# A transformer block pair on one core: the high weights meet high and low activations in one 512-column matmul, and experts are chosen in seven pieces

## The chip, the cores and the metric

The kernel runs on one core of one Trainium2 chip. A core has TensorE (PE, matrix products into PSUM), VectorE (DVE), ScalarE (ACT), GpSimd (POOL), SyncE (SP, which here only starts DMAs) and 16 DMA engines. The metric is the device time of the whole program in microseconds (us). The kernel before was timed three times.

## The reference

A sequence of 256 tokens of width 2048 goes through two blocks in float32. The parts that matter here:

```python
# first block
h = rms_norm(x, norm_mix_g) * (1.0 + sc1) + sh1
u, q, k, v, ga, gb = split(h @ w_in)
merged = sigmoid(ga) * (s5_branch(u) @ w_proj_ssm) + sigmoid(gb) * (moba_attention(q, k, v) @ w_proj_attn)
x = x + g1 * (merged @ w_out)
h2 = rms_norm(x, norm_mlp_g) * (1.0 + sc2) + sh2
x = x + g2 * (square(relu(h2 @ w_ff1)) @ w_ff2)          # width 2048 -> 8192 -> 2048
x = rms_norm(x, norm_final_g)
# second block: hybrid_mixer (its last step is y @ w_out), gated and added to x, then peer_ffn
q = (hf @ wq).reshape(T, 8, 2, 128)                      # 8 heads, two halves
s = einsum('thpd,hpkd->thpk', q, keys)                   # 128 keys in each half
v1, i1 = top_k(s[:, :, 0], 16); v2, i2 = top_k(s[:, :, 1], 16)
cand = v1[..., :, None] + v2[..., None, :]               # 256 candidates of a token and head
vals, pick = top_k(cand, 16); g = softmax(vals)          # 16 of 16384 experts in each head
act = gelu(einsum('td,thkd->thk', hf, down[eidx])) * g
out = einsum('thk,thkd->td', act, up[eidx])
```

The vectors `sh`, `sc`, `g1`, `g2` come from `silu(c) @ w_ada + b_ada` (2048 by 12288, once in each block).

## The kernel before

**Matrix products.** Activations stay in SBUF with features on the partitions and the 256 tokens (T) along the free side. Weights come from HBM as 606 panels of 1024 by 128 numbers (512 KB) that SP loads into six buffers (`raw`). Each weight w is split in two for a product near float32 accuracy: ACT writes `w_hi` (a copy rounded to the type fp32r, `split_to`, L963), DVE writes `w_lo` = w - w_hi (`rest_to`, L1416). The activations are split in the same way (`opa_hi`, `opa_lo`; `opb_hi`, `opb_lo`). `panel` on PE walks the eight 128-row blocks b of a panel and issues three matmuls of 256 columns for each: w_hi by hi, w_hi by lo, w_lo by hi, all summed in columns 0 to 255 of one PSUM bank. Two panels make one group j, a block of 128 output features, in bank j % 4. PE waits for `w_lo` of each panel; ACT and DVE are told to keep three panels ahead (`AHEAD`), `w_hi` has four buffers (`HI`), and a bank is written again when whoever takes it has counted it as free (`FREED`, `wait_freed`).

**Who takes a group.** For w_out, w_ff2 and the second block's w_out (`add_gated`, L1780) DVE adds the bank, times a gate, to the residual `x_res`. For w_ff1 (`hidden`, L1173) ACT takes relu of the bank into `mix` (two buffers), squares it and writes `opb_hi`; DVE then writes `opb_lo` = mix - opb_hi (L1795). The feed-forward runs in four quarters q of 16 w_ff1 groups and 16 w_ff2 groups. Panels 32 (w_out) + 256 (both w_ff) + 32 (second w_out) are the 320 that the change touches.

**Beside it.** DVE also works through the modulation vectors: `ada_steps` (L1434) multiplies a loaded 512 KB piece by a scalar and adds it to an accumulator. `on_beat` spreads 64 such steps over 48 groups (one or two in each, none in the last few), called behind the taking of each group of w_out and of the feed-forward. POOL loads the pieces into four buffers.

**Choice of experts.** `choose(part)` on DVE (L2022 and behind) finds for some heads of one half c of the tokens the 16 best keys of each half, the 16 best of 256 candidates, and their expert numbers (`idx_t`); `PARTS` lists the pieces: heads 0 to 3 and 4 to 7 of tokens 0 to 127, then all eight heads of tokens 128 to 255. `soften` (ACT, exp) and `normalise` (DVE) make their weights. POOL then gathers 4 x 128 rows for all 128 tokens at once (1 MB each): 128 `down` picks and 128 `up` picks for c = 0, then the same for c = 1, into 14 slots; a slot is free once its pick is used. DVE takes a dot product with each `down` pick (L2090); of the `up` picks it adds four of five with a scalar (L2110) and PE takes every fifth (`BY_PE`) with a diagonal that ACT writes. `choose(0)` and `choose(1)` run ahead of the first dot product, `choose(2)` at `up` pick 88 of c = 0. POOL may start pick n only when the piece with its expert numbers is there (L1393).

## Time and profile before

| | us |
|---|---|
| median of three runs | 3714.97 (3707.54 to 3715.55) |
| the profiled execution | 3720.47 |
| its span, first to last instruction | 3717.7 |
| PE busy | 2381.7 |
| DVE busy | 2835.5 |
| ACT busy | 989.6 |
| DMA, mean rate over the span | 287 GB/s |

The profile is of one execution. Its page gives the busy time of each engine, the span in 40 equal slices (each digit the busy share in tenths; PEclk is the clock granted to PE in tenths of full speed) and groups of instructions. The trace behind it answers for any stretch: rows of a timeline (start us, duration us, engine, line, operation, out<-in, partitions x elements, count, and in brackets the idle time before it and what ended that), and rows of stretches (busy time of each engine in a stretch, granted clock, DMA share, GB/s). Records of matmuls overlap, so their rate is read from start to start and not from their durations.

### The profile page before, as it was taken

Reading aid. Unit: us, or ns where it says so; the run is one execution under the profiler, and the core shown is the slowest. Engines: PE = TensorE matmul, PEld = TensorE weight load, DVE = VectorE, ACT = ScalarE, POOL = GpSimd, SP = SyncE. Lnnn points to the kernel's source line nnn. Section 1 sums busy time; section 2 is a strip of 40 time slices with the busy share of each in tenths; the row PEclk is TensorE's granted clock in tenths of the full one; section 3 lists DMA queues with packets and bytes.
Section 4 is the critical chain, followed back from the end, with each engine's and each line's share of the span. In section 5 each row is a group of like instructions: output and inputs, shape, how many; then the busy total and the mean of one; then the engine's idle time right before and its main releaser. Section 6 shows DMA issues by size and latency. Waiting matters only on the chain.

```text
span 3717.7 us, 42305 instructions
## 1 busy us (share of the span) xinstructions
PE 2381.7 (64%) x17026; PEld 2148.6 (58%) x17026; DVE 2835.5 (76%) x3221; ACT 989.6 (27%) x1444; POOL 1256.5 (34%) x975
## 2 busy tenths in 40 slices
...
PEclk6588999999999999999988799855567665555766
...
GB/s 268 189 104 146 342 299 252 339 256 283 269 317 231 319 318 232 317 304 148 161 136 125 1 125 153 108 427 427 427 428 427 414 293 425 427 427 428 427 427 351
DMA packets 223563, 1068.74 MB, mean 287 GB/s; under 512 B 24328, under 2 KB 30472, under 8 KB 157448
## 3 DMA queue, kind: packets, MB, share of 16 engines
...
HBM read 1062.28 MB, written 3.67 MB: 287 GB/s over the span
## 4 chain that ended last, share of the span: by engine, by line
PE 52%; POOL 17%; DMA 12%; DVE 12%; issue 5%; ACT 2%; POOLq 0%; SPq 0%; DVEq 0%; ACTq 0%
PE ps L488 51%; POOL wide L1400 7%; POOL wide_b L1400 5%; DMA raws<-in_up,idx_t 4%; POOL raws L1400 4%; DMA wide_b<-in_up,idx_t 3%; DMA wide<-in_up,idx_t 2%; DVE a_acc L1434 2%; DMA a_acc<-in_up,idx_t 2%; POOL a_acc L1400 1%; DMA a_raws<-in_ada 1%; DVE a_raws L2016 1%; ACT acts L1033 1%; DVE a_raws L2013 1%; DVE ssm_w L1644 1%
## 5 line engine op out<-in xcount | busy, mean ns | idle before, releaser
L1416 DVE TENSOR_TENSOR raws_r<-raws,w_hi 128x1024 fp32r<-128x1024 f32 x606 | 731.4, 1221 | 419.3 <-ACT w_hi L963 418.4
L488 PE MATMUL ps<-opa_hi,w_hi 128*128 128x256 f32 x3152 | 911.0, 289 | 58.6 <-DVE raws_r L1416 32.6
L488 PE MATMUL ps<-opa_lo,w_hi 128*128 128x256 f32 x3152 | 901.9, 286 | 0.0
L488 PE MATMUL ps<-opa_hi,raws_r 128*128 128x256 f32 x3152 | 901.4, 286 | 0.0
L963 ACT ACTIVATE w_hi<-raws 128x1024 fp32r<-128x1024 f32 x606 | 638.8, 1058 | 729.5 <-PE ps L488 547.9
L488 PEld LDWEIGHTS ps<-opa_hi,w_hi 128*128 128x128 f32 x3152 | 615.8, 195 | 64.6 <-issue 46.3
L488 PEld LDWEIGHTS ps<-opa_lo,w_hi 128*128 128x128 f32 x3152 | 615.8, 195 | 0.7 <-issue 0.2
L488 PEld LDWEIGHTS ps<-opa_hi,raws_r 128*128 128x128 f32 x3152 | 615.3, 195 | 0.0
L1316 POOL DMA_DIRECT2D a_raws<-in_ada x320 | 169.7, 530 | 1196.0 <-DVE a_acc L1434 937.2
L488 PE MATMUL ps<-opb_hi,w_hi 128*128 128x256 f32 (+1 forms) x1680 | 487.9, 290 | 24.1 <-DVE opb_lo L1996 14.8
L1434 DVE SCALAR_TENSOR_TENSOR a_acc<-a_raws,csil,a_acc 128x1024 f32<-128x1024 f32 x360 | 472.1, 1345 | 21.7 <-DMA a_raws<-in_ada 21.6
L488 PE MATMUL ps<-opb_lo,w_hi 128*128 128x256 f32 (+1 forms) x1680 | 482.6, 287 | 0.0
L488 PE MATMUL ps<-opb_hi,raws_r 128*128 128x256 f32 (+1 forms) x1680 | 482.4, 287 | 0.0
L488 PE MATMUL ps<-wide,mix 128*128 128x512 f32 x176 | 130.8, 912 | 521.4 <-DMA wide<-in_up,idx_t 521.4
L488 PEld LDWEIGHTS ps<-wide,mix 128*128 128x128 f32 x176 | 50.5, 302 | 600.7 <-issue 600.7
L1400 POOL DMA_INDIRECT raws<-in_down,idx_t x56 | 110.5, 1973 | 756.3 <-DVE idx_t L2050 725.3
L488 PEld LDWEIGHTS ps<-opb_hi,w_hi 128*128 128x128 f32 x1680 | 332.6, 198 | 25.5 <-issue 21.0
L488 PE MATMUL ps<-wide_b,mix 128*128 128x512 f32 x112 | 82.5, 905 | 402.2 <-DMA wide_b<-in_up,idx_t 402.2
L488 PEld LDWEIGHTS ps<-opb_lo,w_hi 128*128 128x128 f32 x1680 | 332.7, 198 | 0.7
L488 PEld LDWEIGHTS ps<-opb_hi,raws_r 128*128 128x128 f32 x1680 | 332.5, 198 | 0.0
L488 PEld LDWEIGHTS ps<-wide_b,mix 128*128 128x128 f32 x112 | 32.2, 303 | 452.0 <-issue 452.0
L2090 DVE CUSTOM_DVE_ANT_0 wide<-wide,acts 128x2048 f32<-128x2048 f32 x110 | 248.8, 2288 | 9.9 <-DMA wide<-in_down,idx_t 6.0
...
## 6 DMA issues: line engine op xcount, KB each, us to landing
raws<-in_w SPq DMA_DIRECT2D x606, 512.0 KB, 4.3
a_raws<-in_ada POOLq DMA_DIRECT2D x320, 512.0 KB, 5.7
...
wide<-in_up,idx_t POOLq DMA_INDIRECT x111, 28.4
...
```

The lines of the kernel that those rows point to most:

```text
L488: return nc.tensor.matmul(out, lhs, rhs, start=start, stop=stop)
L963: nc.scalar.activation(w_hi[p % HI][:, :, :].rearrange("p b n -> p (b n)"), raw[p % RAW], ACT.Copy).then_inc(S["hi"], 1)
L1033: link(nc.scalar.activation(tmp[:, k, :], tmp[:, k, :], ACT.Identity, bias=shift[:, k:k + 1], scale=gain[:, k:k + 1]), wait=False)
L1316: pool.dma_start(a_raw[q % HALVES], a["ada"][q]).then_inc(bland[q % HALVES], 16)
L1400: pool.indirect_dma_start(gslot[slot], None, table, bass.IndirectOffsetOnAxis(ap=idx_t[:, pick:pick + 1], axis=0)).then_inc(S[f"gat{slot}" ...
L1416: TT(w_lo[p % RAW].rearrange("p b n -> p (b n)"), raw[p % RAW], w_hi[p % HI][:, :, :].rearrange("p b n -> p (b n)").bitcast(F32), ALU.subt ...
L1434: ins = STT(a_acc[:, h, :], a_raw[h], c, a_acc[:, h, :], ALU.mult, ALU.add)
L1644: link(V.tensor_tensor_scan(r1[:, g, :], m, w1[:, g, :], 0.0, ALU.mult, ALU.add), wait=False)
L2013: link(V.max(values[:, u, s8_], src[:, u, :]), wait=False)
L2016: link(V.max_index(indices[:, u, s8_], values[:, u, s8_], src[:, u, :]), wait=False)
L2090: V.tensor_tensor_reduce(gslot[n % SLOTS], gslot[n % SLOTS], hf[c], 1.0, 0.0, ALU.mult, ALU.add, dots_t[:, at:at + 1]).then_inc(S["used"], 1)
```

## The change

Four things are done.

1. `opa_hi` and `opa_lo` become the halves of one tensor `opa_both` (for each feature block 256 high columns and then 256 low ones), likewise `opb_both`. In 320 panels `wide_panel` issues two matmuls for each block: w_hi by both halves, 512 columns, a whole bank, and w_lo by the high half, 256 columns, into columns 0 to 255.
2. Whoever takes the group adds the bank's halves. `add_gated` does two dependent multiply-adds instead of one. In `hidden` ACT copies the second half to `mix`, DVE adds the first half (semaphores `fhalf`, `fsum`; the bank is free from `fsum` on), and ACT's relu, square and rounded copy of a group follow one group later, as does DVE's `opb_lo`.
3. `PARTS` has seven pieces: heads 0-1, 2-4, 5-7 for c = 0 and four pairs of heads for c = 1. Two are chosen ahead of the first dot product, the third at dot product 8, the four pairs at `up` picks 8, 34, 60 and 86 of c = 0.
4. `soften` and `normalise` follow the pieces; the first choice waits for one copied bank of scores instead of two.

```diff
@@ -129,18 +129,18 @@
-    at, count = 0, {"a": 0, "d": 0}
+    at, count = 0, {"a": 0, "d": 0, "f": 0}
     for name, n, by in (
         ("u", 8, "a"), ("head0", 3, "a"), ("glu", 8, "a"), ("heads", 21, "a"), ("merge", 16, "d"), ("out", 16, "d"),
-        ("ff1_0", 16, "a"), ("ff2_0", 16, "d"), ("ff1_1", 16, "a"), ("ff2_1", 16, "d"),
-        ("ff1_2", 16, "a"), ("ff2_2", 16, "d"), ("ff1_3", 16, "a"), ("ff2_3", 16, "d"),
+        ("ff1_0", 16, "f"), ("ff2_0", 16, "d"), ("ff1_1", 16, "f"), ("ff2_1", 16, "d"),
+        ("ff1_2", 16, "f"), ("ff2_2", 16, "d"), ("ff1_3", 16, "f"), ("ff2_3", 16, "d"),
         ("in2", 37, "a"), ("out2", 16, "d"), ("wq", 16, "d"),
...
             count[by] += 1
-            FREED.append(("freed_" + by, count[by]))
+            FREED.append(({"a": "freed_a", "d": "freed_d", "f": "fsum"}[by], count[by]))
...
 _groups()
@@ -173,7 +173,10 @@
 SLOTS = 14
-PARTS = ((0, 0, 4), (0, 4, 8), (1, 0, 8))
+PARTS = ((0, 0, 2), (0, 2, 5), (0, 5, 8), (1, 0, 2), (1, 2, 4), (1, 4, 6), (1, 6, 8))
+FIRST_OF = {256 * c + 16 * h0: part for part, (c, h0, h1) in enumerate(PARTS)}
+SOFT_AT = {24: 3, 49: 4, 74: 5, 99: 6}
+CHOSEN_AT = {8: 3, 34: 4, 60: 5, 86: 6}
 BY_PE = range(4, PICKS, 5)
...
@@ -309,8 +312,8 @@
-        opa_hi = sb("opa_hi", [P, DC, T], F32R)
-        opa_lo = sb("opa_lo", [P, DC, T], F32R)
+        opa_both = sb("opa_both", [P, DC, 2, T], F32R)
+        opa_hi, opa_lo = opa_both[:, :, 0, :], opa_both[:, :, 1, :]
         acts = sb("acts", [P, 32, T])
...
@@ -499,12 +503,33 @@
+            def wide_panel(p, bank, both, c0, first, last, ready=None):
+
+                hi, lo = w_hi[p % HI], w_lo[p % RAW]
+                pe.wait_ge(S["lo"], p + 1)
+                for b in range(8):
+                    if ready and (c0 + b) % ready[2] == 0:
+                        pe.wait_ge(S[ready[0]], ready[1] + (c0 + b) // ready[2] + 1)
+                    final = last and b == 7
+                    if final:
+                        mm(ps[:, bank, 0:T], lo[:, b, :], both[:, c0 + b, 0, :], False, False)
+                    m = mm(ps[:, bank, :], hi[:, b, :], both[:, c0 + b, :, :].rearrange("p x t -> p (x t)"),
+                           first and b == 0, final)
+                    if not final:
+                        m = mm(ps[:, bank, 0:T], lo[:, b, :], both[:, c0 + b, 0, :], False, False)
+                m.then_inc(S["panel"], 1)
+
             opa, opb = (opa_hi, opa_lo), (opb_hi, opb_lo)
-            def linear(p0, g0, rhs, groups=16, ready=None, beat=None, swapped=False, sums=None, between=None):
+            def linear(p0, g0, rhs, groups=16, ready=None, beat=None, swapped=False, sums=None, between=None,
+                       both=None):
...
+                    if both is not None:
+                        wide_panel(halves(p0, j, swapped)[x], j % 4, both, 8 * x, x == 0, x == 1,
+                                   ready if j == 0 else None)
+                        return
                     panel(halves(p0, j, swapped)[x], ps[:, j % 4, 0:T], rhs, 8 * x, x == 0, x == 1,
...
@@ -778,11 +803,13 @@
             wait_freed(pe, GRP["out"] - 1)
-            linear(PAN["out"], GRP["out"], opa, ready=("op", 12, 4), beat=0, swapped=True, sums=plain_sums(4))
+            linear(PAN["out"], GRP["out"], opa, ready=("op", 12, 4), beat=0, swapped=True, sums=plain_sums(4),
+                   both=opa_both)
             for q in range(4):
-                linear(PAN["ff"] + 64 * q, GRP[f"ff1_{q}"], opa, ready=("op", 16, 2), beat=16 + 32 * q, swapped=q == 0)
+                linear(PAN["ff"] + 64 * q, GRP[f"ff1_{q}"], opa, ready=("op", 16, 2), beat=16 + 32 * q, swapped=q == 0,
+                       both=opa_both)
                 linear(PAN["ff"] + 64 * q + 32, GRP[f"ff2_{q}"], opb, ready=("hid", 16 * q, 1),
-                       beat=32 + 32 * q, sums=double_sums(20) if q == 3 else None)
+                       beat=32 + 32 * q, sums=double_sums(20) if q == 3 else None, both=opb_both)
             ada_sums(5)
...
             linear(PAN["in2"], GRP["in2"], opa, ready=("op", 24, 2), swapped=True)
@@ -901,7 +928,7 @@
                 m.then_inc(S["yss"], 1)
-            linear(PAN["out2"], GRP["out2"], opb, ready=("yop", 0, 8), sums=plain_sums(52))
+            linear(PAN["out2"], GRP["out2"], opb, ready=("yop", 0, 8), sums=plain_sums(52), both=opb_both)
             linear(PAN["wq"], GRP["wq"], opa, ready=("op", 32, 2), swapped=True)
...
             wait_freed(pe, GRP["wq"] + 15)
@@ -1175,10 +1202,17 @@
                         act.wait_ge(S["hid"], n - 1)
-                    nc.scalar.activation(mix[:, n % 2, :], ps[:, j % 4, 0:T], ACT.Relu).then_inc(S["freed_a"], 1)
-                    wait_freed(act, GRP[f"ff1_{q}"] + j)
-                    link(nc.scalar.activation(mix[:, n % 2, :], mix[:, n % 2, :], ACT.Square))
-                    nc.scalar.activation(opb_hi[:, j, :], mix[:, n % 2, :], ACT.Copy).then_inc(S["ffc"], 1)
+                    nc.scalar.activation(mix[:, n % 2, :], ps[:, j % 4, T:2 * T], ACT.Copy).then_inc(S["fhalf"], 1)
+                    if j:
+                        square_hidden(n - 1)
+                square_hidden(16 * q + 15)
+
+            def square_hidden(n):
+
+                act.wait_ge(S["fsum"], n + 1)
+                link(nc.scalar.activation(mix[:, n % 2, :], mix[:, n % 2, :], ACT.Relu))
+                link(nc.scalar.activation(mix[:, n % 2, :], mix[:, n % 2, :], ACT.Square))
+                nc.scalar.activation(opb_hi[:, n % 16, :], mix[:, n % 2, :], ACT.Copy).then_inc(S["ffc"], 1)
...
                 hidden(q)
@@ -1291,15 +1325,15 @@
-            soften(0)
-            soften(1)
+            for part in range(3):
+                soften(part)
             for c in range(2):
-                if c:
-                    soften(2)
                 act.wait_ge(S["used"], c * (2 * PICKS - EACH) + PICKS)
...
                 for i, k in enumerate(BY_PE):
+                    if c == 0 and k in SOFT_AT:
+                        soften(SOFT_AT[k])
                     if c * EACH + i >= 2:
...
                     A(mix[:, i % 2, 0:P], ident, ACT.Identity,
@@ -1392,8 +1426,8 @@
                 slot, table, pick = n % SLOTS, a["up"] if up else a["down"], c * PICKS + k
-                if n in (0, 64, 2 * PICKS):
-                    pool.wait_ge(S["eix"], 1 + (0, 64, 2 * PICKS).index(n))
+                if n in FIRST_OF:
+                    pool.wait_ge(S["eix"], 1 + FIRST_OF[n])
                 if n >= SLOTS:
...
                     pool.wait_ge(S[name], count)
@@ -1777,7 +1811,8 @@
                     dve.wait_ge(S["panel"], done)
-                    STT(x_res[:, j, :], ps[:, j % 4, 0:T], modcol(gate, 1, j), x_res[:, j, :], ALU.mult,
+                    link(STT(x_res[:, j, :], ps[:, j % 4, 0:T], modcol(gate, 1, j), x_res[:, j, :], ALU.mult, ALU.add))
+                    STT(x_res[:, j, :], ps[:, j % 4, T:2 * T], modcol(gate, 1, j), x_res[:, j, :], ALU.mult,
                         ALU.add).then_inc(S["freed_d"], 1)
...
                         on_beat(beat + j)
@@ -1787,14 +1822,22 @@
+            def hidden_lo(n):
+
+                dve.wait_ge(S["ffc"], n + 1)
+                TT(opb_lo[:, n % 16, :], mix[:, n % 2, :], opb_hi[:, n % 16, :].bitcast(F32), ALU.subtract).then_inc(
+                    S["hid"], 1)
+
             for q in range(4):
                 for j in range(16):
-                    n = 16 * q + j
-                    rest_to(halves(PAN["ff"] + 64 * q, j, q == 0)[1] + 1 + AHEAD)
-                    dve.wait_ge(S["ffc"], n + 1)
-                    TT(opb_lo[:, j, :], mix[:, n % 2, :], opb_hi[:, j, :].bitcast(F32), ALU.subtract).then_inc(
-                        S["hid"], 1)
+                    n, done = 16 * q + j, halves(PAN["ff"] + 64 * q, j, q == 0)[1] + 1
+                    rest_to(done + AHEAD)
+                    dve.wait_ge(S["fhalf"], n + 1)
+                    TT(mix[:, n % 2, :], mix[:, n % 2, :], ps[:, j % 4, 0:T], ALU.add).then_inc(S["fsum"], 1)
+                    if j:
+                        hidden_lo(n - 1)
                     on_beat(16 + 32 * q + j)
+                hidden_lo(16 * q + 15)
                 add_gated(PAN["ff"] + 64 * q + 32, 5, 32 + 32 * q)
...
             TT(gain[:, :], gain[:, :], col("norm_final_g", 0, DC), ALU.mult).then_inc(S["gn"], 1)
@@ -2060,12 +2103,10 @@
-            dve.wait_ge(S["scc"], 2)
+            dve.wait_ge(S["scc"], 1)
             choose(0)
...
             choose(1)
-            normalise(0)
-            normalise(1)
...
@@ -2086,19 +2127,24 @@
                         finish(0)
+                    if c == 0 and k == 8:
+                        choose(2)
+                        for part in range(3):
+                            normalise(part)
                     dve.wait_ge(S[f"gat{n % SLOTS}"], 16 * (n // SLOTS + 1))
...
                 if c:
-                    normalise(2)
+                    for part in range(3, 7):
+                        normalise(part)
                 cc = slice(c * P, c * P + P)
...
                     n, at = (2 * c + 1) * PICKS + k, c * PICKS + k
-                    if c == 0 and k == 88:
-                        choose(2)
+                    if c == 0 and k in CHOSEN_AT:
+                        choose(CHOSEN_AT[k])
                     if k in BY_PE:
...
                     slot, weight = gslot[n % SLOTS], dots_t[:, at:at + 1]
```

On PE, where w_ff2's first quarter ends and w_ff1's second quarter begins, stood (`opa`, `opb`: activations; `raws_r`: the low weights):

```order
L488 MATMUL ps<-opb_hi,w_hi3 128x256
L488 MATMUL ps<-opb_lo,w_hi3 128x256
L488 MATMUL ps<-opb_hi,raws_r 128x256
L488 MATMUL ps<-opa_hi,w_hi0 128x256 [waits s_op,s_lo,s_freed_d]
L488 MATMUL ps<-opa_lo,w_hi0 128x256
L488 MATMUL ps<-opa_hi,raws_r 128x256
```

and now stands:

```order
L492 MATMUL ps<-opb_both,w_hi3 128x512
L492 MATMUL ps<-opb_both,raws_r 128x256 x2
L492 MATMUL ps<-opb_both,w_hi3 128x512
L492 MATMUL ps<-opa_both,w_hi0 128x512 [waits s_op,s_lo,s_freed_d]
L492 MATMUL ps<-opa_both,raws_r 128x256
```

Three records of 256 columns have become one of 512 and one of 256; the waits stand where they stood.

On DVE, from one group of w_ff1's second quarter to the next, stood:

```order
L1434 SCALAR_TENSOR_TENSOR a_acc<-a_raws,csil,a_acc 128x1024 [waits s_ada,s_bland1]
L1434 SCALAR_TENSOR_TENSOR a_acc<-a_raws,csil,a_acc 128x1024 [waits s_ada,s_bland2]
L1416 TENSOR_TENSOR raws_r<-raws,w_hi3 128x1024 [waits s_hi]
L1416 TENSOR_TENSOR raws_r<-raws,w_hi0 128x1024 [waits s_hi]
L1795 TENSOR_TENSOR opb_lo<-mix,opb_hi 128x256 [waits s_ffc]
```

and now stands:

```order
L1468 SCALAR_TENSOR_TENSOR a_acc<-a_raws,csil,a_acc 128x1024 [waits s_ada,s_bland0]
L1468 SCALAR_TENSOR_TENSOR a_acc<-a_raws,csil,a_acc 128x1024 [waits s_ada,s_bland1]
L1450 TENSOR_TENSOR raws_r<-raws,w_hi3 128x1024 [waits s_hi]
L1450 TENSOR_TENSOR raws_r<-raws,w_hi0 128x1024 [waits s_hi]
L1836 TENSOR_TENSOR mix<-mix,ps 128x256 [waits s_fhalf]
L1828 TENSOR_TENSOR opb_both<-mix,opb_both 128x256 [waits s_ffc]
```

The sum of the halves (L1836) is new, and the subtraction behind it (L1828) belongs to the group before. On DVE in the `up` picks of c = 0 stood, at pick 88:

```order
L2110 SCALAR_TENSOR_TENSOR acts<-wide,a_raws,acts 128x2048 x3
L2013 MAX a_raws<-acts 128x8 x16
L2016 MAX_INDEX a_raws<-a_raws,acts 128x8 x16
L2020 MATCH_REPLACE acts<-a_raws,acts 128x128 x16
L2013 MAX a_raws<-acts 128x8 x16
```

and now stands, at pick 8 and in the same form at 34, 60 and 86:

```order
L2156 SCALAR_TENSOR_TENSOR acts<-wide,a_raws,acts 128x2048 x5
L2156 SCALAR_TENSOR_TENSOR acts<-wide_b,a_raws,acts 128x2048
L2056 MAX a_raws<-acts 128x8 x4
L2059 MAX_INDEX a_raws<-a_raws,acts 128x8 x4
L2063 MATCH_REPLACE acts<-a_raws,acts 128x128 x4
L2056 MAX a_raws<-acts 128x8 x4
```

One run over 16 score rows has become four runs over four, with `up` picks between them.

## Rows read from the trace of the kernel before

**Rows 1.** The page: PE's granted clock and the DMA rate in 40 slices.
```profile
PEclk6588999999999999999988799855567665555766
...
GB/s 268 189 104 146 342 299 252 339 256 283 269 317 231 319 318 232 317 304 148 161 136 125 1 125 153 108 427 427 427 428 427 414 293 425 427 427 428 427 427 351
```

**Rows 2.** Stretches: busy us (x instructions) of PE, PEld, DVE, ACT, POOL; clock; DMA.
```profile
947.26:1716.80 769.54, 769.54 (x6267) 767.80 (x6267) 555.43 (x559) 351.52 (x478) 88.40 (x167) 0.98 0.81 288
...
1270.00:1293.00 23.00, 23.00 (x194) 23.00 (x194) 18.50 (x19) 8.46 (x9) 3.18 (x6) 1.00 0.90 320
...
383.00:480.00 97.00, 96.84 (x804) 96.58 (x805) 85.79 (x119) 45.42 (x80) 16.86 (x32) 1.00 0.93 340
```

**Rows 3.** Timeline of PE at full clock: 256, 256 (float32) and 30 columns.
```profile
1299.93 0.28 PE L488 MATMUL ps<-opb_hi,w_hi 128*128 128x256 f32 x1
1300.05 0.28 PE L488 MATMUL ps<-opb_lo,w_hi 128*128 128x256 f32 x1
...
1694.16 0.81 PE L488 MATMUL ps<-acts,ones 128*128 128x256 f32 x3
...
1694.16 1.02 PE L488 MATMUL ps<-acts,ones 128*128 128x256 f32 x4
...
1928.82 0.26 PE L488 MATMUL ps<-opb_hi,raws_r 128*128 128x30 f32 x1
1928.93 0.26 PE L488 MATMUL ps<-opb_hi,w_hi 128*128 128x30 f32 x1
```

**Rows 4.** Timeline of DVE in w_ff2 (1240 to 1246) and in w_ff1 (1195).
```profile
1240.77 2.47 DVE L1434 SCALAR_TENSOR_TENSOR a_acc<-a_raws,csil,a_acc 128x1024 f32<-128x1024 f32 x2
1243.16 2.49 DVE L1416 TENSOR_TENSOR raws_r<-raws,w_hi 128x1024 fp32r<-128x1024 f32 x2
1246.13 0.48 DVE L1780 SCALAR_TENSOR_TENSOR x_res<-ps,mod,x_res 128x256 f32<-128x256 f32 x1 [0.48 <-PE ps L488]
...
1195.61 0.43 DVE L1795 TENSOR_TENSOR opb_lo<-mix,opb_hi 128x256 fp32r<-128x256 f32 x1 [1.82 <-ACT opb_hi L1181]
```

**Rows 5.** Waits from 950 to 1700: total us, times, longest.
```profile
ACT w_hi L963 <- PE ps L488: 231.5, 153, 15.3
...
ACT w_hi L963 <- DMA raws<-in_w: 66.5, 30, 3.6
```

**Rows 6.** Timeline of DVE and POOL at the first two choices.
```profile
2374.52 1.65 DVE L2013 MAX8 a_raws<-acts 128x8 f32<-128x128 f32 x8 [10.23 <-ACT acts L1284]
...
2402.91 1.64 DVE L2013 MAX8 a_raws<-acts 128x8 f32<-128x128 f32 x8
2403.86 1.02 POOL L1400 DMA_INDIRECT raws<-in_down,idx_t  x1 [725.26 <-DVE idx_t L2050]
...
2432.73 2.29 DVE L2090 CUSTOM_DVE_ANT_0 raws<-raws,acts 128x2048 f32<-128x2048 f32 x1
...
2434.95 2.29 DVE L2090 CUSTOM_DVE_ANT_0 raws<-raws,acts 128x2048 f32<-128x2048 f32 x1
```

**Rows 7.** The third choice: timeline of DVE and POOL, then stretches (columns as in Rows 2).
```profile
2941.73 3.19 DVE L2013 MAX8 a_raws<-acts 128x8 f32<-128x128 f32 x16
...
2994.63 4.80 DVE L2110 SCALAR_TENSOR_TENSOR acts<-wide,a_raws,acts 128x2048 f32<-128x2048 f32 x2
2997.24 2.99 POOL L1400 DMA_INDIRECT wide<-in_up,idx_t  x1 [52.14 <-DVE acts L2110]
2999.53 2.35 DVE L2110 SCALAR_TENSOR_TENSOR acts<-wide_b,a_raws,acts 128x2048 f32<-128x2048 f32 x1
...
2441.00:2941.00 500.00, 99.89 (x136) 38.89 (x136) 443.68 (x322) 7.83 (x20) 386.18 (x212) 0.59 1.01 427
...
2960.00:2980.00 20.00, 8.27 (x14) 3.03 (x12) 19.69 (x79) 0.80 (x2) 0.00 (x0) 0.81 0.58 243
2980.00:3000.00 20.00, 0.00 (x0) 0.00 (x0) 19.48 (x13) 0.00 (x0) 2.76 (x1) 0.53 0.00 0
3000.00:3020.00 20.00, 6.09 (x8) 2.38 (x8) 19.17 (x9) 0.40 (x1) 17.45 (x9) 0.59 0.96 388
```

11 lines of the change are left out of this document (6 added, 5 removed).

## The prediction

> **What bounds the kernel now.** I read the page's slices first. PE runs at nearly full clock up to about 2360 us and then at half of it or a little more; the DMA rate is at most 342 GB/s before that point and near 427 GB/s behind it, but for slices at 1, at 293 and the last [rows 1]. So there are two kernels in one: matrix products up to 2364 us and gathers behind them, each with a bound of its own. The stretches tell which. In the feed-forward, 947.26 to 1716.80, PE is busy for 769.54 of 769.54 us, DVE for 555.43 and ACT for 351.52 [rows 2]; what ACT waits for there is mostly PE (231.5 us) and only now and then a weight load (66.5 us in 30 waits) [rows 5]. PE is the bound, and its cost there is the distance from one record's start to the next: 1299.93 to 1300.05, 0.12 us [rows 3]. A group of two panels is 48 records, 5.76 us. In the gathers the bound is the DMA: 427 GB/s over 500 us [rows 7], that is 1,048,576 bytes / 427 GB/s = 2.456 us for each of 512 gathers, with DVE at 443.68 of those 500 us. Its stalls are the only thing to win there.
>
> **Part 1: the wide matmul.** In the 320 panels 2560 blocks go from three records to two. PE streams as many columns as before (768), so the gain is what a record costs beyond its columns. Three rows bound it. A record of 256 columns takes 0.120 us at the 2.4 GHz level (granted clock 1.00), where 256 / 2.4 GHz is 0.107 [rows 3]. A record of 30 columns still takes 0.11 (1928.82 to 1928.93) [rows 3]: there the columns are nothing, so about 0.11 us is the price of loading new weights, beside the stream of the record before. Last, the float32 sums over `ones`: one more record adds 1.02 - 0.81 = 0.21 us [rows 3]. Each has a weight load too, but streams each column twice, 512 column times, 0.213 us. So a stream of 0.213 us hides the load whole, while one of 0.107 us about equals the load and costs 0.120. The new record has exactly those 512 column times. I take 0.215 for it and, since its neighbour has 256 columns and must hide the next load as today, 0.120 for that: 0.335 us a block against 0.360. The ends: the 13 ns stick to each record (0.213 + 0.013 = 0.227, block 0.347), or to each 256 columns (0.240, block 0.360, no gain); on the other side the narrow record falls to the 0.11 of a load (block 0.325). I choose 0.335 because the row with the same stream length shows it.
>
> 2560 x 0.025 = 64.0 us. Where PE stands at the 1.2 GHz level (short stretches behind each modulation sum and at the start of the second w_out; I estimate 25 us of the 320 panels) the stream is longer than the load anyway and nothing is won: 25 / 5.76 groups x 0.4 = 1.7, so -62.3 us.
>
> What a rule says to this: the Trainium skill (TensorE: Matmul & The Clock Gate, "Back-to-back issue gap") gives a warm gap of N / 2.4 + 2.5 ns. By it three records of 256 take 327 ns and the new pair 325, so merging would bring 2560 x 2.5 ns = 6 us and not 64. The trace does not agree on the start: it has 120 where the rule has 109.
>
> **Does anybody else become the bound?** A group will take 16 x 0.335 = 5.36 us. DVE is next. In a dense stretch of w_ff2 it is busy for 18.50 of 23 us [rows 2], 4.63 us of each 5.76: two `w_lo` (2.49), one or two modulation steps (2.47 for two), one take of 0.48 [rows 4]. The second multiply-add depends on the first: 0.48 plus some 0.10 for the semaphore (estimated from L2110, which waits for itself: from 2994.63 to 2999.53 are two records, 2.45 us each, of which one lasts 2.35 [rows 7]). 4.63 + 0.58 = 5.21 us, 97% of 5.36. In w_ff1 the added sum costs about the 0.43 of L1795 [rows 4]: 5.06 us. Today DVE waits 1.82 us for ACT there [rows 4]; now it needs `mix` from ACT, adds, and waits for ACT's relu, square and copy of the group before, some 1.0 us while it runs in step with PE. 6.1 us would be more than 5.36; but DVE may fall behind PE by up to three panels (8 us), and as soon as it is 1 us behind ACT's part is done when DVE arrives. So it falls behind by about 1 us in each quarter and then keeps step: no cost. Queued behind this new wait on DVE are the modulation steps and the next two `w_lo`; PE needs those only three panels (8.0 us) after the group ends, and they are there after some 6. The last `opb_lo` of a quarter now stands behind a group's modulation steps, about 4.4 us after the last panel; w_ff2 needs it in its 16th block, after 15 x 0.335 = 5.0 us. The DMA must bring 3.5 x 524,288 bytes in 5.36 us, 342 GB/s; 340 was held for 97 us with PE at 96.84 of 97 and a DMA share of 0.93 [rows 2]. Near the edge, but loads have four panels of room. What is left: +0.58 us at the end of each of the three residual stages, where the norm waits for the last take (+1.7), and +2 for the two swapped starts, where groups end each 2.7 us and DVE falls behind. Part 1 in all: -62.3 + 3.7 = -58.6 us.
>
> **Part 2: the choice.** `choose` with four heads runs from 2374.52 to 2402.91, where the next begins, 28.4 us, with eight from 2941.73 to 2994.63, 52.9 us [rows 6, 7]. So 6.1 us a head and 3.9 fixed; two heads 16.1, three 22.2. The third choice is where time is lost: in 2960 to 3020 the DMA moved 243, 0 and 388 GB/s where 427 fit [rows 7], so 8.6 + 20.0 + 1.8 = 30.4 us idle, and some 1 us more behind it. Four pieces of 16.1 us against 14 slots x 2.456 = 34.4 us of cover: a piece alone stalls nothing. DVE must also catch up between them: it takes four of five picks at 2.45 us [rows 7], 9.8 us of each 12.28, so 26 picks win back 12.9 us of the 16.1. Its lag at the end of the pieces is 16, 19, 23 and 26 us, below the 34.4 less some 5 from an issue to its data (POOL issues at 2997.24, and 388 of 427 GB/s from 3000 on mean that data flow from 3001.8 [rows 7]). So all 31 us come back, with 4 us to spare; the 42 picks that remain win back 21. ACT's `soften` stands before the diagonals of picks 24, 49, 74 and 99, 13 or more picks (32 us) behind its piece; nobody waits.
>
> **The start.** The first gather goes out at 2403.86 [rows 6]. With two heads it goes out at 2391, 12.3 us earlier for the two heads and some 0.6 for the earlier score bank. But DVE then has 22.2 us of second choice, eight dot products (2434.95 - 2432.73 = 2.22 us each [rows 6], 17.8) and 22.2 us of third choice with three normalisations (I estimate 2.1 from the gap of about 30 us from 2402.91 to 2432.73, of which 28.4 are the choice): from 2390 on that is 64.3 us, so dot product 8 begins at 2454. POOL has 14 slots and 8 that became free, 22 gathers or 54.0 us of data, counted from 2391; slot 23 is free at 2454 + 2.2 = 2456.5. Counted without the delay from issue to data, which both have, gather 22 comes at 2456.5 and comes today at 2403.9 + 54.0 = 2457.9. The gain of the early start is thus given back by a new gap of 2456.5 - 2445.0 = 11.5 us: 1 us is left, between -2 and +4, and I count 0. Part 2: -31 us.
>
> **Sum.** -58.6 - 31 = -89.6 against the profiled execution's own 3720.47: 3630.9. That execution lies 5.5 us above the median of the three, so against the median 3714.97 the forecast is **3625 us**.
>
> **Rivals.** (a) The overhead goes with the record, block 0.347: part 1 is 34 - 1 - 3.7 = 29 us, time 3655. For it: nothing in the trace has new weights, fp32r and 512 columns. Against it: the 0.21 us row. Chance 0.13. (b) It goes with the columns, block 0.360: no gain on PE, 3.7 us of longer takes, -27 us in all, 3688. For it: no row has fp32r at more than 256 columns. Chance 0.07. By the gap of the page named above it would be 6 us less, 3682. (c) DVE becomes the bound: if links and waits bring its group to 5.6 us, 0.16 instead of 0.4 is won in 160 groups, 3625 + 38 = 3663; if only in the 80 groups of w_ff2 and w_out, 3644. For it the 97% above, against it that in 383 to 480 PE lost 0.16 of 97 us beside a DVE busy for 85.79 [rows 2], and that a DVE which has fallen behind waits no more. Chance 0.14. (d) The choices' lag passes 30 us, or the stall at the start is longer: 5 to 15 us back, 3630 to 3640. Chance 0.10, inside the range. (e) Slower: an fp32r record of 512 columns runs like a float32 one, which took 0.21 us for 256 [rows 3], two column times for each column: 0.427 a record, block 0.547: +0.187 x 2560 = +479 us, 4160. It decides from 0.251 us a record on, where it has eaten part 2. Against it: the 256-column fp32r records stream at one column time. Chance 0.03. (f) The narrow record falls to 0.11, block 0.325: PE group 5.2 us, just DVE's; -20 us, 3605. Chance 0.07. My forecast keeps 0.46.
>
> **Range and chances.** 3604 to 3664 holds the forecast, (a), (d), (f) and most of (c), 0.86. The measurement tells about 0.2% (7 us) from no change. All cases but (e) lie over 25 us below 3715; for what I overlooked (a longer exchange between ACT and DVE, a DMA near its limit) I keep 0.02 for no change and 0.01 more for slower. Faster 0.94, same 0.02, slower 0.04.
>
> **What the profile after would show.** In the feed-forward: starts 0.215 us apart behind a record of 512 columns and 0.12 behind one of 256; groups at 5.36 us; PE busy without a gap over some 720 us instead of 769.5; DVE at 93 to 97% in w_ff2. If starts are right but PE has gaps that `w_lo` ends, it is (c). In the gathers: no slice below 420 GB/s around the four pieces, and one new gap of about 12 us some 54 us behind the first gather. Wrong would be: 0.227 or 0.24 behind the wide record, a gap at the third or fourth piece, or PE waiting for `hid` at the start of w_ff2.

## The result and the profile after

| | before | after |
|---|---|---|
| median, us | 3711.26 (3704.02 to 3715.55) | 3667.43 (3664.56 to 3670.80) |
| profiled execution / its span, us | 3720.47 / 3717.7 | 3670.80 / 3669.0 |

The ratio is 0.9884, with a 95% interval of 0.9864 to 0.9905: the changed kernel is faster by 44 us (1.2%). The forecast was 3625 us, 90 less than before; what was measured has its sign and about half its size, and the time lies 3.4 us above its range. Both parts of the sum can be read apart. All times here and below are of executions at the usual clock; one of the six of one_head below ran at a lower one (3763.13 us, clock 0.716) and is left out.

**The products.** The timeline of PE in w_ff2 of the kernel after, at full clock (start, duration, engine and line, operation, count), answers to the first two of [rows 3]:

```profile
1299.97 0.28 PE L492 MATMUL ps<-opb_both,raws_r 128*128 128x256 f32 x1
1300.08 0.40 PE L492 MATMUL ps<-opb_both,w_hi 128*128 128x512 f32 x1
1300.31 0.28 PE L492 MATMUL ps<-opb_both,raws_r 128*128 128x256 f32 x1
1300.43 0.40 PE L492 MATMUL ps<-opb_both,w_hi 128*128 128x512 f32 x1
1300.67 0.28 PE L492 MATMUL ps<-opb_both,raws_r 128*128 128x256 f32 x1
1300.79 0.40 PE L492 MATMUL ps<-opb_both,w_hi 128*128 128x512 f32 x1
1301.03 0.28 PE L492 MATMUL ps<-opb_both,raws_r 128*128 128x256 f32 x1
1301.14 0.40 PE L492 MATMUL ps<-opb_both,w_hi 128*128 128x512 f32 x1
```

Read starts, not durations: from 1300.08 to 1301.14 are three blocks, 1.06 us, so 0.353 each, and from a wide record to its narrow one it is 0.23 or 0.24 us where 0.215 was forecast. A whole stage is the better ruler, since it averages over 256 blocks. One window over the w_ff1 of the third quarter, of before and then of after (busy us and instructions of PE, PEld, DVE, ACT, POOL; clock; DMA share; GB/s; the windows run from the first to the last low-weights record). The last line is a whole w_ff2 of after, that of the second quarter:

```profile
1321.05:1412.85 91.80, 91.80 (x768) 91.80 (x766) 69.09 (x70) 50.58 (x77) 11.11 (x21) 1.00 0.86 309
```
```profile
1310.21:1400.08 89.87, 89.87 (x511) 77.96 (x509) 74.47 (x84) 54.07 (x89) 11.08 (x21) 1.00 0.89 313
```
```profile
1219.53:1309.75 90.22, 90.22 (x513) 78.26 (x512) 81.10 (x90) 36.43 (x39) 12.67 (x24) 1.00 0.90 330
```

PE has no gap in any. Before, 255 blocks lie between the two records: 91.80 / 255 = 0.360 us. After, the last narrow record stands before its wide one, so a wide record is missing: (89.87 + 0.24) / 255 = 0.3534. PEld, the weight loads, was busy all the time and is now busy for 77.96 us: the loads no longer fill the stage, and yet it is hardly shorter. DVE is at 83% in w_ff1 and at 90% (81.10 of 90.22 us) in w_ff2, the DMA at 0.89 and 0.90, and PE waits for neither of them, so neither took the gain.

**The gathers.** The slices of the page after, to be read beside [rows 1]:

```profile
PEclk6588999999999999999988789855557765555777
...
GB/s 271 189 109 134 346 295 252 330 290 263 267 326 235 329 322 243 323 312 153 160 142 132 1 115 151 143 363 427 427 428 427 427 410 425 427 428 427 428 427 343
```

The slice with 293 is gone; a 410 stands there. The timelines of PE, POOL and DVE at the start, and stretches of 20 us (columns as above):

```profile
2355.23 0.28 PE L492 MATMUL ps<-raws_r,opb_both 128*128 128x128 f32 x1
...
2368.01 1.02 POOL L1434 DMA_INDIRECT raws<-in_down,idx_t  x1 [708.52 <-DVE idx_t L2093]
...
2407.02 1.25 DVE L2056 MAX8 a_raws<-acts 128x8 f32<-128x128 f32 x6
...
2408.21 0.95 POOL L1434 DMA_INDIRECT wide<-in_down,idx_t  x1 [0.30 <-issue]
...
2431.31 2.29 DVE L2135 CUSTOM_DVE_ANT_0 wide<-wide,acts 128x2048 f32<-128x2048 f32 x1
...
2433.88 2.74 POOL L1434 DMA_INDIRECT wide<-in_down,idx_t  x1 [24.72 <-DVE a_raws L2135]
```
```profile
2400.00:2420.00 20.00, 0.00 (x0) 0.00 (x0) 19.69 (x75) 0.00 (x0) 7.94 (x5) 0.50 1.01 427
2420.00:2440.00 20.00, 0.00 (x0) 0.00 (x0) 19.24 (x37) 1.52 (x2) 5.51 (x3) 0.50 0.40 153
2440.00:2460.00 20.00, 0.00 (x0) 0.00 (x0) 20.00 (x19) 0.00 (x0) 17.26 (x10) 0.50 1.00 407
...
2940.00:2960.00 20.00, 9.54 (x14) 3.40 (x12) 19.17 (x9) 0.80 (x2) 15.90 (x7) 0.75 0.93 370
2960.00:2980.00 20.00, 11.13 (x14) 4.50 (x15) 19.17 (x9) 0.40 (x1) 17.41 (x9) 0.59 1.00 408
```

What is missing to 427 GB/s is 12.8 us and 0.9 us, together 13.8 before rounding, at the start and 2.7 + 0.9 = 3.6 us behind the fourth piece of the second half. The balance of the two profiled executions, taken at the last record of the keys (2378.34 us before, 2355.23 after): products -23.1; the first gather follows 12.8 us behind it instead of 25.5, so -12.7; new gap +13.8; stalls 30.4 [rows 7] to 3.6, so -26.8; together -48.8, and the spans differ by 48.7.

### The profile page after: what moved, and what is told of

It is laid out like the page before. It is cut to its first block, busy times and chain, and to the rows that moved or that the text cites. A ratio compares the mean times of both kernels' runs of the same rounds, so it can differ in the third digit from the quotient of the medians.

```text
span 3669.0 us, 37493 instructions
## 1 busy us (share of the span) xinstructions
PE 2355.8 (64%) x14466; PEld 2004.2 (55%) x14466; DVE 2916.4 (79%) x3453; ACT 1009.1 (28%) x1512; POOL 1281.0 (35%) x975
## 4 chain that ended last, share of the span: by engine, by line
PE 51%; DVE 17%; POOL 15%; DMA 10%; issue 5%; ACT 2%; DVEq 0%; SPq 0%; POOLq 0%; ACTq 0%
PE ps L492 50%; POOL wide L1434 7%; DVE acts L2156 4%; POOL wide_b L1434 4%; POOL raws L1434 3%; DMA wide<-in_up,idx_t 2%; DMA raws<-in_up,idx_t 2%; DMA wide_b<-in_up,idx_t 2%; DVE a_acc L1468 2%; POOL a_acc L1434 1%; DMA a_raws<-in_ada 1%; DVE a_raws L2059 1%; DMA wide<-in_down,idx_t 1%; DMA a_acc<-in_up,idx_t 1%; DVE a_raws L2056 1%
## 5 line engine op out<-in xcount | busy, mean ns | idle before, releaser
L492 PE MATMUL ps<-opa_both,w_hi 128*128 128x256 f32 (+1 forms) x5024 | 1152.3, 318 | 60.6 <-DVE raws_r L1450 33.2
L492 PEld LDWEIGHTS ps<-opa_both,w_hi 128*128 128x128 f32 x5024 | 835.6, 194 | 119.7 <-issue 47.6
L492 PE MATMUL ps<-opa_both,raws_r 128*128 128x256 f32 x3152 | 885.0, 285 | 0.0
L492 PE MATMUL ps<-opb_both,w_hi 128*128 128x512 f32 (+2 forms) x2080 | 615.8, 362 | 24.3 <-DVE opb_both L2039 14.8
L492 PEld LDWEIGHTS ps<-opa_both,raws_r 128*128 128x128 f32 x3152 | 611.2, 194 | 7.4
L492 PE MATMUL ps<-opb_both,raws_r 128*128 128x256 f32 (+1 forms) x1680 | 466.3, 285 | 0.0
L492 PEld LDWEIGHTS ps<-opb_both,w_hi 128*128 128x128 f32 x2080 | 377.2, 198 | 76.5 <-issue 21.0
L492 PEld LDWEIGHTS ps<-opb_both,raws_r 128*128 128x128 f32 x1680 | 328.7, 196 | 7.0
L2156 DVE SCALAR_TENSOR_TENSOR acts<-wide,a_raws,acts 128x2048 f32<-128x2048 f32 x88 | 206.9, 2351 | 39.8 <-DMA wide<-in_up,idx_t 32.2
L1434 POOL DMA_INDIRECT wide<-in_down,idx_t x110 | 215.8, 1962 | 59.3 <-issue 32.9
## 6 DMA issues: line engine op xcount, KB each, us to landing
x_res<-in_xT SPq DMA_DIRECT2D x1, 2048.0 KB, 12.7
```

The source lines that it names most:

```text
L492: return nc.tensor.matmul(out, lhs, rhs, start=start, stop=stop)
L1434: pool.indirect_dma_start(gslot[slot], None, table, bass.IndirectOffsetOnAxis(ap=idx_t[:, pick:pick + 1], axis=0)).then_inc(S[f"gat{slot}" ...
L2156: STT(p_acc[c], slot, weight, p_acc[c], ALU.mult, ALU.add).then_inc(S["used"], 1)
```

## Experiments

Theories on the wide record: **fixed**, 13 ns of each record whatever its columns, which was rival (a); **columns**, a price that grows with them, rival (b); **traffic**, SBUF shared with DVE, ACT and DMA; **bank**, the narrow record adds where the wide one has just written; **same weights**, 0.215 true only where the weights don't change. For the gathers: a stall that follows from DVE's lag, or one that something else makes.

**bench.** Behind the last result, PE issues trains of 96 records on operands copied there for it (an excerpt; the DVE, ACT and DMA work that runs beside some trains is left out):

```diff
+            def b_512(r):
+                return [(0, 0, 512, w(i), x(i)) for i in range(r)]
...
+            main = (b_pair, b_three, b_512)
...
+            for phase in range(3):
+                for make in main:
+                    m = run(make(96))
+                m.then_inc(S["bph"], 1)
```

> After the last result PE issues trains of 96 records each on operands that nobody writes, first alone, then beside DVE and ACT, then beside DMA loads, then beside all; the distance between starts at the 2.4 GHz level is read. What the changed kernel's extra 0.018 us of a 512-column record (0.233 instead of 0.215) belongs to: (R) a fixed price of a record, 13 ns, as in rival (a): 512 columns alone 0.227, 384 columns 0.173, 256 columns 0.120, and the same in all four surroundings. (C) a price that grows with the columns: 512 alone 0.233, 384 about 0.175 to 0.180, 256 about 0.120, 128 at the price of a weight load, 0.11. (T) the traffic of the other engines and of the DMA on SBUF: alone 0.215 beside 0.120, the pair 0.335; 0.233 only beside DVE, ACT or DMA. (B) the narrow record adds into the bank half that the wide one has just written: with the narrow one in another bank or in the other half the pair falls from 0.350 to 0.335, and 512-column records in a row take 0.215. (S) my forecast's value, 0.215, is true of records with the same weights only: the train with one weight tile shows 0.215, the one with new weights 0.233.

Stretches of its trace, each from the first start of a train to its last, so 95 distances (the counts include a record or two of the neighbours). In order: the pair, three records of 256 as before, 512 alone, 256, 384, 320, 512 with one weight tile; then the pair beside DVE and ACT, beside DMA loads, beside all:

```profile
3780.03:3796.74 16.71, 16.71 (x97) 14.51 (x95) 0.00 (x0) 0.00 (x0) 0.00 (x0) 1.00 0.00 1
3796.97:3808.38 11.41, 11.41 (x97) 11.40 (x96) 0.00 (x0) 0.00 (x0) 0.00 (x0) 1.00 0.01 1
3808.49:3830.05 21.56, 21.56 (x98) 17.84 (x96) 0.00 (x0) 0.00 (x0) 0.00 (x0) 1.00 0.00 1
3830.27:3841.67 11.40, 11.40 (x97) 11.39 (x96) 0.00 (x0) 0.00 (x0) 0.00 (x0) 1.00 0.00 0
3841.79:3858.26 16.47, 16.47 (x98) 16.47 (x96) 0.00 (x0) 0.00 (x0) 0.00 (x0) 1.00 0.00 1
3878.27:3892.20 13.93, 13.93 (x97) 13.93 (x95) 0.00 (x0) 0.00 (x0) 0.00 (x0) 1.00 0.00 1
3903.01:3924.61 21.60, 21.60 (x97) 17.89 (x97) 0.00 (x0) 0.00 (x0) 0.00 (x0) 1.00 0.00 1
3991.74:4008.46 16.72, 16.72 (x97) 14.53 (x95) 16.00 (x14) 16.04 (x16) 0.00 (x0) 1.00 0.01 1
4041.99:4058.70 16.71, 16.71 (x96) 14.51 (x95) 0.39 (x1) 0.00 (x0) 7.77 (x15) 1.00 0.83 319
4092.24:4108.95 16.71, 16.71 (x96) 14.51 (x95) 15.99 (x14) 15.97 (x16) 5.59 (x11) 1.00 0.83 316
```

21.56 / 95 = 0.2269 us for 512 columns, 16.47 / 95 = 0.1734 for 384, 13.93 / 95 = 0.1466 for 320, 11.40 / 95 = 0.1200 for 256. Less columns / 2.4 GHz that leaves 13.6, 13.4, 13.3 and 13.3 ns: fixed. One length of this run does not fit: 448 columns took 206.6 ns, 20 over their columns. The surroundings change nothing (16.71 or 16.72 us each time), and one weight tile changes nothing (its 95 distances: 0.2274). So traffic, columns and same weights fall. The train of pairs ends with its last pair turned round, so its 95 distances are 47 behind a wide record and 48 behind a narrow one, and a pair is (16.71 - 0.12) / 47 = 0.3530 us, 6.1 ns more than 0.2269 + 0.1200. (The 0.3518 and the 4.9 ns in the expectations below are 16.71 divided by 47.5 pairs, which leaves this out.) With the narrow record in another bank it stayed 16.71 us, with it in the upper half of the same bank it took 16.42, 0.3468 a pair, the two records' own prices. That last difference I took for a finding.

**bench2, upper, turned.** The second set of trains asks what the extra of the pair is and where my 0.215 came from. Two kernels try it in place.

Upper, in both places where the narrow record is issued:

```diff
-                        m = mm(ps[:, bank, 0:T], lo[:, b, :], both[:, c0 + b, 0, :], False, False)
+                        m = mm(ps[:, bank, T:2 * T], lo[:, b, :], both[:, c0 + b, 0, :], False, False)
```

Turned:

```diff
-                    final = last and b == 7
-                    if final:
+                    final, turned = last and b == 7, b % 2
+                    if turned:
...
-                    if not final:
+                    if not turned:
```

> More trains of 96 records behind the last result, with nothing beside them. The first trains gave 0.2269 us for 512 columns and 0.1200 for 256, that is columns / 2.4 GHz + 13.3 ns, but 0.3518 for the pair, 0.0049 more than the two, and only 0.3458 with the narrow record in the upper half of the bank. Alternation (A): the 4.9 ns come from each change from wide to narrow or back; then wide, narrow, narrow, wide in turn has half as many and gives 0.349 a pair. Address (D): they come from the narrow record's place in the bank: records of 256 columns alone at offset 256 then take less than 0.120, or the order changes nothing (0.352 low, 0.346 high). Moving operand (M): they come from reading the first half of an operand that the record before has just read whole; with the second half as operand the pair in the low half of the bank falls to 0.346. Float32: my forecast took 0.215 for 512 column times from float32 records over ones. If a float32 record has no 13 ns because it is one of the two passes of the same matmul, a train of float32 products of 256 columns takes 2 x 0.215 also with new weights for each; if the ones (same weights for all) made it, it takes 2 x 0.227.

Stretches of bench2: wide, narrow, narrow, wide; the plain pair; float32 products of 256 columns with new weights (192 records, 191 distances); the pair with the narrow record in the upper half.

```profile
3845.08:3861.57 16.49, 16.49 (x97) 14.39 (x95) 0.00 (x0) 0.00 (x0) 0.00 (x0) 1.00 0.00 1
3787.72:3804.43 16.71, 16.71 (x96) 14.52 (x95) 0.00 (x0) 0.00 (x0) 0.00 (x0) 1.00 0.00 1
3912.42:3953.64 41.22, 41.22 (x193) 36.28 (x191) 0.00 (x0) 0.00 (x0) 0.00 (x0) 1.00 0.00 1
3828.14:3844.85 16.71, 16.71 (x97) 14.51 (x95) 0.00 (x0) 0.00 (x0) 0.00 (x0) 1.00 0.00 0
```

The upper half is at 16.71 now: the same train had 16.42 in the run before, so the place in the bank was not its cause. Theories D and M fall too: narrow records alone take 0.120 us at either offset tried, and the pair stays at 16.71 whichever half of the operand the narrow record reads. The turned order takes 16.49; it too has 47 distances behind wide records and 48 behind narrow ones, so a block is (16.49 - 0.12) / 47 = 0.3483 us, 1.4 ns over 0.2269 + 0.1200. So the extra comes with strict alternation, as theory A said, but the turned order loses 4.7 of the 6.1 ns where A had it lose half. Float32 records with new weights take 41.22 / 191 = 0.2158 us, 213.3 + 2.5 ns: it is the type that made my 0.215, not the constant ones. Why an fp32r record pays 13.3 ns and a float32 one 2.5 stays open.

> The changed kernel, but low weights times high operand are added into the upper half of the bank, where high weights times low operand already is, instead of the lower. The sum is the same. If the train's 6 ns a block (0.3518 to 0.3458) hold in the kernel, 2560 x 0.006 = 15 us: 3652 us, ratio 0.984, and a stage of 32 panels falls from 89.86 to 88.3 us. If something else than the records sets the pace in the kernel (weights halves of DVE, loads), the ratio stays at 0.988.

3669.90 us (3665.30 to 3672.86), ratio 0.9883 (0.9868 to 0.9898): no difference to the changed kernel, and the stage of 32 panels takes the same 89.87 us. The bank theory is dead in place as well.

> The changed kernel with the order of the two records turned in every second block: wide, narrow, narrow, wide. By (A) 2.5 ns a block less, 6 us: 3661 us, ratio 0.9868, a stage of 32 panels 89.2 us. By (D) or (M) no change: 0.988 and 89.9 us.

3661.66 us (3659.21 to 3663.66), ratio 0.9858 (0.9843 to 0.9873), against 0.9884: about 9 us less, with intervals that just overlap. The stage says it more sharply. The same w_ff1 of the third quarter in the run of upper, then of turned:

```profile
1306.46:1396.33 89.87, 89.87 (x511) 77.94 (x510) 74.49 (x84) 54.06 (x89) 11.13 (x21) 1.00 0.88 314
```
```profile
1305.09:1393.68 88.59, 88.59 (x511) 77.31 (x509) 75.27 (x85) 54.09 (x89) 11.13 (x21) 1.00 0.89 321
```

(88.59 + 0.24) / 255 = 0.3484 us a block for 0.3534: the trains had 0.3483 and 0.3530, so the long stages run as the trains do, within 0.4 ns. In w_out of the second block, where sums over ones stand between the groups, turned and changed kernel take the same time (96.08 and 96.06 us): there the plain order already has starts 0.23 and 0.12 apart in the timeline. So the plain alternation can fall into a slower beat of three pairs (in the long stages and most trains) or into a faster one (behind such sums, and in one train of bench); the turned order took 0.348 in its train and in the long stages, close to the faster beat's 0.3468. What sets the beat is not settled, and wasn't tried further.

**pieces_only, wide_only.** Each part of the change alone: the kernel before with the seven pieces, and the changed kernel with the three choices of before.

pieces_only, against the kernel before, with what follows from it:

```diff
-PARTS = ((0, 0, 4), (0, 4, 8), (1, 0, 8))
+PARTS = ((0, 0, 2), (0, 2, 5), (0, 5, 8), (1, 0, 2), (1, 2, 4), (1, 4, 6), (1, 6, 8))
```

wide_only, against the changed kernel, likewise:

```diff
-CHOSEN_AT = {8: 3, 34: 4, 60: 5, 86: 6}
+CHOSEN_AT = {88: 2}
```

> The kernel before with the choice in seven pieces and nothing else of the change. If the two parts add up, the trace of the changed kernel gives it -25.6 us: ratio 0.993 to the kernel before, and the wide matmul the other -23. If the wide matmul gained more than its stages show (because the gathers lost something to it), this one is at -31 us or more, 0.992 and below. If the part of the pieces is worth more on the changed kernel than alone, it is at -20 us or less, 0.995 and above.

3689.79 us (3686.32 to 3691.62), ratio 0.9935 (0.9914 to 0.9956).

> The changed kernel's wide products with the choice of the kernel before (four heads, four heads, eight heads before pick 88). By the fixed 13.3 ns of each record and 4.9 ns a block for the changes between wide and narrow, a block is 0.3510 us and the end of the products comes 23 us earlier: 3689 us, ratio 0.9938. If the gathers take some of it back, 3695 us or more, 0.995 and above; if the parts of the change are worth more together than each alone (0.9884 against 0.9935 for the pieces alone), it is above 0.995 too.

3696.05 us (3695.80 to 3700.04), ratio 0.9942 (0.9928 to 0.9957). 0.9935 x 0.9942 = 0.9877, and 0.9884 was measured: the parts add up within their intervals, 24 us for the pieces and 22 us for the products. The ratio is the one expected (0.9938); the 3696 us are above the 3689 expected because the kernel before took 3718.51 us beside it, 7 more than in the table above. wide_only also has its third choice still in one piece, and the stall with it, 14.7 + 17.2 + 1.8 = 33.7 us (before 30.4):

```profile
2940.00:2960.00 20.00, 6.16 (x8) 2.38 (x8) 19.70 (x68) 0.40 (x1) 0.00 (x0) 0.59 0.27 113
2960.00:2980.00 20.00, 0.00 (x0) 0.00 (x0) 19.44 (x12) 0.00 (x0) 6.49 (x3) 0.50 0.17 59
2980.00:3000.00 20.00, 6.21 (x8) 2.38 (x8) 18.81 (x8) 0.40 (x1) 17.56 (x9) 0.59 1.00 388
```

**third_at_64, spread.** The choice of the heads 5 to 7 is needed only by gather 80. It moves from dot product 8 to 64; then the four pieces of the second half are spread too.

```diff
-                    if c == 0 and k == 8:
+                    if c == 0 and k == 64:
```

spread, besides:

```diff
-SOFT_AT = {24: 3, 49: 4, 74: 5, 99: 6}
-CHOSEN_AT = {8: 3, 34: 4, 60: 5, 86: 6}
+SOFT_AT = {29: 3, 64: 4, 99: 5, 124: 6}
+CHOSEN_AT = {12: 3, 46: 4, 80: 5, 112: 6}
```

> The changed kernel with the third choice before dot product 64 instead of 8; gather 80, the first that needs it, is issued only when slot 66 comes free. If the 13.8 us of missing data rate from 2420 to 2460 us are only the stall that follows from DVE being 34 us behind, they come back: 3654 us, ratio 0.985 to the kernel before. If the stall moves to dot product 64 (DVE has then had 64 x 0.24 = 15 us to catch up, and the choice takes 24), 5 us or less of it stays. If the gap has another cause (the queue of gathers, POOL), nothing comes back and the ratio stays 0.988.

3660.60 us (3655.77 to 3663.57), ratio 0.9850 (0.9828 to 0.9873). The ratio is the one expected, but its interval overlaps the changed kernel's, and the medians differ by 7 us only. The traces are sharper: from the issue of the first gather to that of the last it is 1245.2 us where the changed kernel has 1255.5 (2368.01 to 3623.53), so the move is worth 10 us. The gap at the start is gone, 1.4 us are missing at dot product 64, and some of it comes back at the later pieces, presumably because DVE now reaches them with more lag:

```profile
2420.00:2440.00 20.00, 0.00 (x0) 0.00 (x0) 20.00 (x19) 0.00 (x0) 17.18 (x9) 0.50 1.01 427
2860.00:2880.00 20.00, 9.43 (x12) 3.72 (x13) 19.07 (x22) 0.92 (x3) 9.92 (x5) 0.61 0.95 387
2880.00:2900.00 20.00, 8.11 (x14) 3.08 (x12) 19.17 (x9) 0.80 (x2) 17.56 (x9) 0.79 1.00 390
2920.00:2940.00 20.00, 8.65 (x13) 3.14 (x11) 19.11 (x53) 0.92 (x3) 8.02 (x7) 0.76 0.96 404
2940.00:2960.00 20.00, 11.05 (x14) 4.57 (x15) 19.17 (x9) 0.40 (x1) 17.56 (x9) 0.59 0.99 382
```

1.9 + 1.7 + 1.1 + 2.1 = 6.8 us at the later pieces in place of 3.6.

> As the one with the third choice before dot product 64, and the four pieces of the second half before picks 12, 46, 80 and 112 instead of 8, 34, 60 and 86. If the 3.6 us missing from 2940 to 2980 us are DVE's summed lag at the fourth piece, they come back too: 3650 us, ratio 0.984, and no stretch of 20 us between the first gather and the last below 420 GB/s. If they belong to the piece itself, they stay and the time is that of the other.

3653.25 us (3649.31 to 3655.45), ratio 0.9833 (0.9811 to 0.9854). From the first gather to the last it is 1242.4 us, 3 less than third_at_64; the rest of the 7 us between the two medians is not shown to belong to the change. The pieces of the second half leave no gap any more; what is left stands at dot product 64, 0.7 + 0.9 = 1.6 us:

```profile
2540.00:2560.00 20.00, 0.00 (x0) 0.00 (x0) 19.21 (x43) 1.53 (x2) 4.32 (x2) 0.50 1.00 411
2560.00:2580.00 20.00, 0.00 (x0) 0.00 (x0) 20.00 (x19) 0.00 (x0) 17.26 (x10) 0.50 1.01 408
...
2960.00:2980.00 20.00, 9.77 (x15) 3.56 (x13) 18.92 (x62) 2.21 (x4) 10.77 (x9) 0.74 1.01 428
```

**upper_spread, turned_spread, one_head.** Combinations. one_head chooses one head first, then three, two and two.

Against turned_spread:

```diff
-PARTS = ((0, 0, 2), (0, 2, 5), (0, 5, 8), (1, 0, 2), (1, 2, 4), (1, 4, 6), (1, 6, 8))
+PARTS = ((0, 0, 1), (0, 1, 4), (0, 4, 6), (0, 6, 8), (1, 0, 2), (1, 2, 4), (1, 4, 6), (1, 6, 8))
...
-                    if c == 0 and k == 64:
-                        choose(2)
+                    if c == 0 and k in (48, 82):
+                        choose(2 if k == 48 else 3)
```

> Upper half of the bank together with the third choice before dot product 64 and the other four before picks 12, 46, 80 and 112. If the two are independent, 3653 - 15 = 3638 us, ratio 0.979. If an earlier end of the products is given back at the gathers, 3645 to 3653 us, ratio 0.982.

3653.52 us (3650.60 to 3658.40), ratio 0.9838 (0.9825 to 0.9852): that of spread, as it has to be when the upper half is worth nothing. The expectation was wrong in its first term.

> Both finds together: the two records of every second block in turned order (0.3461 us a block in the run with it alone, 9 us less in all) and the choices before dot product 64 and picks 12, 46, 80 and 112 (14 us less). If independent: 3653 - 9 = 3644 us, ratio 0.981. If only one of the two counts, 0.9833 to 0.986.

3646.67 us (3642.22 to 3651.89), ratio 0.9808 (0.9795 to 0.9820): the two finds add up, as expected (0.981).

> As the version with both finds, but the first choice is of one head (10 us instead of 16), then three before the first dot product and two each before dot products 48 and 82; the first gather goes out 6 us earlier. DVE's lag at the end of the last of these is 17 + 22 - 0.24 x 82 + 16 - 5 = about 30 us where 34.4 less 5 are covered: if the lag counts as in the case of the fourth piece, 1 to 3 us of stall come there, and 3 to 5 us are won: 3640 us, ratio 0.980. If the early start is given back whole, as in the changed kernel, no difference to the version with both finds.

3643.09 us (3641.45 to 3644.49), ratio 0.9795 (0.9782 to 0.9808). The median is 3.6 us lower than that of turned_spread and the intervals overlap; that one_head is faster isn't shown by its times. Its trace has both sides of the trade. The first gather goes out at 2351.67, 6.7 us behind the keys instead of 12.8, and from there to the last gather it is 1245.5 us instead of turned_spread's 1241.6: 6.1 us won, 3.9 lost, 2 left. Data are missing behind the choice at dot product 82 (3.7 us) and behind picks 12 and on (1.3 + 1.6 us):

```profile
2580.00:2600.00 20.00, 0.00 (x0) 0.00 (x0) 19.55 (x31) 1.51 (x2) 9.04 (x5) 0.50 0.89 347
2720.00:2740.00 20.00, 9.51 (x13) 3.85 (x14) 19.08 (x35) 0.63 (x2) 5.96 (x3) 0.70 0.98 400
2740.00:2760.00 20.00, 8.70 (x13) 3.21 (x11) 19.17 (x9) 0.80 (x2) 17.56 (x9) 0.67 1.00 393
```

## Why the prediction was right in kind and wrong in size

**What bounds the kernel: right.** In the changed kernel's feed-forward (931.95 to 1693.40) PE is busy for 759.67 of 761.45 us, and its one longer stop (1.55 us, for `w_lo`, at the swapped start of the first quarter) was 1.03 us before. Behind the keys the DMA is at 427 GB/s in every run but for the gaps named.

**The wide record, 0.215 us: wrong, and this is the step that failed.** I had three prices for a stream of 512 column times and chose the one from the float32 row of [rows 3], on the argument that a long stream hides the weight load whole. The load is hidden, as PEld's 77.96 of 89.87 us show, but it wasn't what the 13 ns were: they are there at 320, 384 and 512 columns alike. A float32 record has the same length of stream and pays 2.5 ns; an fp32r record pays 13.3. What decided was the type, and I had matched the rows by the stream's length. Rival (a) had the right mechanism and 0.347 us; the 0.3530 of the train and the 0.3534 of the long stages have a further 6 ns that no case of mine named, the beat of the alternation. From the first record of each stage to the first of the next one, the ten stages with wide panels take 22.4 us less (2.6 in w_out, 17.6 in the feed-forward, 2.2 in the second w_out); without the 1.5 us that the takes add (below) that is 23.9. Of these 3.6 us are not the records': the two modulation sums inside the feed-forward, whose records did not change, ran from 1128.77 to 1140.10 and from 1418.73 to 1429.89 before (granted clock 0.61 and 0.62) and take 9.48 and 9.39 us now (0.73 and 0.74). So the records gave about 20 us where 62.3 stood. The gap that the Trainium skill (TensorE: Matmul & The Clock Gate, "Back-to-back issue gap") gives for a matmul by itself, N / 2.4 + 2.5 ns, agrees with the float32 records, one of which streams 512 column times (215.8 ns measured), and not with the fp32r ones, which have 13.3 ns in place of its 2.5. What I had worked out from it, that merging saves one fixed gap a block, was right: with 13.3 ns for the gap it gives what rival (a) gave.

**The narrow record at 0.120: right**, 0.117 from it to the next wide record in the train of pairs. Case (f), a block of 0.325, is far from anything measured.

**DVE as the bound: right that it isn't**, but my 97% rested on the 5.36 us group. In w_ff2 DVE works 81.10 / 16 = 5.07 us a group where I had 5.21. Of the 5.64 us that a group now takes this is 90%, and PE waits for none of it, so rival (c) plays no part here; whether it would at 5.36 us was not tested. The chain of takes cost what was said: in the timeline of DVE in w_ff2 the second multiply-add starts 0.52 us behind the first (0.58 in the forecast):

```profile
1293.22 0.48 DVE L1814 SCALAR_TENSOR_TENSOR x_res<-ps,mod,x_res 128x256 f32<-128x256 f32 x1
1293.74 0.48 DVE L1815 SCALAR_TENSOR_TENSOR x_res<-ps,mod,x_res 128x256 f32<-128x256 f32 x1
```

From the end of the last record of a residual stage to the first record of the next it is now 0.48 to 0.52 us longer, three times: 1.5 us for the 1.7 forecast. The added exchange between ACT and DVE in w_ff1 made no gap on PE in the three later quarters.

**The third choice, -31 us: right to 4 us.** 26.8 came back. The missing 3.6 us are at the fourth piece, where I had "4 us to spare". My bound compared the lag at the piece's end (26 us) with 34.4 less 5. What it left out is, I think, that the slot comes free only when the pick behind the piece has been used, another 2.35 us, and that the first pieces begin with some lag of their own; DVE's lag itself was not read from the trace. spread, which gives DVE more picks between the pieces, has no gap there, so it is the summed lag and not the piece.

**The early start, 0 us: right to 1 us**, and for the reason given: 22 gathers, then a gap, 13.8 us instead of 11.5. But I stopped a step early. The same count of slots says that nobody needs the choice before gather 80, so the gap was a matter of where it stands; moving it gave 10 us in the trace.

**Range.** It ended at 3664, taking in rival (a) at 3655 and most of (c), but not a rival (a) together with the small losses of the gathers (3.6 + 1.1 + some tenths at the end) and the 6 ns of the beat. The rivals were priced one by one around the forecast's other terms; two of them at once lie outside.
